# Early input columns at the seam of two blocks, a slot of its own for the lanes' change of tokens, and GpSimd multiplying values with gates

## What is computed

```python
def peer_ffn_2(xn, w_q, sub_keys, u_tab, v_tab):
    ...
        eidx = jnp.take_along_axis(cidx, ci, axis=-1)     # 8 heads x 16 experts a token
        gate = jax.nn.softmax(cs, axis=-1)
        ug = u_tab[eidx]
        act = jax.nn.gelu(jnp.einsum('td,thkd->thk', xb, ug).astype(f32))
        vg = v_tab[eidx]
        return jnp.einsum('thk,thkd->td', (gate * act).astype(vg.dtype), vg)
```

```python
    lam = lax.complex(a_re.astype(f32), a_im.astype(f32))
    dt = jnp.exp(log_dt.astype(f32))[:, None]
    a_bar = jnp.exp(lam * dt)
    b_bar = ((a_bar - 1.0) / lam)[..., None] * lax.complex(b_re.astype(f32), b_im.astype(f32))
```

## Time and profile before

| | before |
|---|---|
| median of 3 runs | 1944.17 us |
| lowest, highest | 1938.46, 1945.6 us |
| profiled execution | 1944.28 us |
| its span on the core | 1942.4 us |
| PE busy | 1879.8 us (97%) |
| DVE busy | 1254.2 us (65%) |
| ACT busy | 495.9 us (26%) |
| POOL busy | 360.3 us (19%) |
| DMA | 619.66 MB, mean 319 GB/s |

### The profile page before, as it was taken

One profiled execution on the slowest core, in us unless ns is written; L12 is line 12 of the kernel. 1 busy time (PEld: TensorE's weight loads), 2 busy tenths in 40 slices (PEclk: granted clock), 3 DMA queues, 4 the chain that ended last, 5 costly groups with the idle time before them and its releaser, 6 DMA issues. The chain is left out here.

```text
span 1942.4 us, 33702 instructions
## 1 busy us (share of the span) xinstructions
PE 1879.8 (97%) x13111; PEld 1757.2 (90%) x13111; DVE 1254.2 (65%) x2927; ACT 495.9 (26%) x1707; POOL 360.3 (19%) x310
## 2 busy tenths in 40 slices
PE   8999999999999999999999989999999999999998
PEld 6877779999999999999988567899999999999998
DVE  6228566998888834434599974339997888444344
ACT  3013302324445310000311024013234454100002
POOL 0000000233333211111000740000332333111110
PEclk9999999999999999999999999999999999999999
DMA  7763369999999999999544120379999999999996
GB/s 307 279 253 128 135 257 371 361 415 414 414 415 414 406 391 414 413 413 414 198 137 145 66 98 1 109 273 349 417 415 414 413 414 414 390 414 413 414 413 242
DMA packets 125373, 619.66 MB, mean 319 GB/s; under 512 B 14812, under 2 KB 17020, under 8 KB 83360
## 3 DMA queue, kind: packets, MB, share of 16 engines
q1 hardware_dynamic: 91264, 382.77, 50.5%
q0 software_dynamic: 31376, 226.27, 28.6%
q10 hardware_dynamic: 2576, 8.48, 1.2%
HBM read 614.84 MB, written 2.62 MB: 318 GB/s over the span
## 5 line engine op out<-in xcount | busy, mean ns | idle before, releaser
L1237 PE MATMUL bank<-expert_coef,ring 128*128 128x152 f32 x4096 | 535.8, 293 | 5.2 <-DMA ring<-in_uv 4.6
L1237 PEld LDWEIGHTS bank<-expert_coef,ring 128*128 128x128 f32 x4096 | 530.4, 190 | 8.9 <-DMA ring<-in_uv 7.6
L1208 PE MATMUL bank<-h,ring 128*128 128x152 f32 x3712 | 498.9, 293 | 4.4 <-DMA ring<-in_ut 4.4
L1208 PEld LDWEIGHTS bank<-h,ring 128*128 128x128 f32 x3712 | 484.8, 190 | 6.2 <-DMA ring<-in_ut 6.0
L1156 POOL DMA_INDIRECT expert_rows<-in_uv,pair_index x208 | 289.4, 1391 | 971.1 <-DVE pair_sum L1528 534.5
L1517 DVE CUSTOM_DVE_ANT_0 expert_rows<-expert_rows,h_tokens 128x1024 f32<-128x1024 f32 x192 | 234.4, 1221 | 213.6 <-DMA expert_rows<-in_uv,pair_index 213.5
L1528 DVE SCALAR_TENSOR_TENSOR pair_sum<-expert_rows,pair_coef,pair_sum 128x1024 f32<-128x1024 f32 x192 | 246.2, 1282 | 45.9 <-ACT pair_coef L1378 44.6
L1376 ACT ACTIVATE pair_act<-pair_dot 128x1 f32<-128x1 f32 x208 | 42.2, 203 | 599.4 <-DVE pair_dot L1517 599.1
L1172 PE MATMUL bank<-h,ring 128*128 128x128 f32 x1024 | 117.1, 275 | 0.0
L1172 PEld LDWEIGHTS bank<-h,ring 128*128 128x128 f32 x1024 | 116.0, 192 | 0.1
L1362 ACT ACTIVATE work<-work,choice 128x128 f32<-128x128 f32 x304 | 97.2, 406 | 0.0
(11 more groups left out here) (414 smaller groups left out, 2058.1 us busy)
## 6 DMA issues: line engine op xcount, KB each, us to landing
ring<-in_uv SPq DMA_DIRECT2D x256, 512.0 KB, 13.1
ring<-in_ut SPq DMA_DIRECT2D x232, 512.0 KB, 14.7
ring<-in_dense SPq DMA_DIRECT2D x92, 1024.0 KB, 4.8
expert_coef<-in_ut SPq DMA_DIRECT2D x24, 512.0 KB, 8.0
ada<-in_ada SPq DMA_DIRECT2D x8, 1024.0 KB, 23.8
ada_late<-in_ada ACTq DMA_DIRECT2D x7, 1024.0 KB, 4.7
ada_late<-in_ada SPq DMA_DIRECT2D x5, 1024.0 KB, 11.8
ada<-in_ada POOLq DMA_DIRECT2D x4, 1024.0 KB, 16.1
```

Of the source, the lines that this page charges most:

```text
L1208: ins = nc.tensor.matmul(k.bank[e % 4][:, 0:DENSE], w[:, kk, :], k.h[:, kk, SPREAD_END:TOK], start=kk == 0, stop=kk == KD - 1)
L1237: ins = nc.tensor.matmul(down_bank(i), w[:, i * P:(i + 1) * P], A[:, e, :], start=e == 0 and i % 3 == 0, stop=e == NB - 1, skip_group_chec ...
```

## The change

It does four things.

1. **Front columns at the seam.** In place of the products that feed nothing, TensorE multiplies the 116 front columns for the first four tiles of the second block's input projection (`EARLY_TILES`), in banks 2 to 5, at the end of `peer_layer` "1". In `block2_inputs` the first four tiles then cover only the other 156 columns.
2. **The S5 factors in layer 1.** Their constants come by a transfer on ScalarE's queue, and their arithmetic (one Exp, two Sin, one Tanh on ScalarE; a chain on VectorE in three parts) is put between late pairs in the down half of layer 1. What `block2_inputs` still does of it are the masks, the input factors, and the tables.
3. **A slot for the turn.** The change of tokens at p = 32 gets a step of its own, `turn_at` = 69, without a pair. Every pair from 32 on comes two tiles later, so `late` becomes 61. The last four pairs before the gates move to other tiles (`PAIR_AT`: 45, 46, 48, 50 become 45, 47, 51, 53). In the down half a gather waits for 59/20 = 2.95 tiles more instead of 3.
4. **GpSimd multiplies.** `weigh` goes from VectorE's program to GpSimd's, where the multiplies that are due stand between the issues of the gathers (`weigh_to`). ScalarE waits for all of them before it widens the first shared tokens.

```diff
+EARLY_TILES, EARLY_BANK = 4, 2
-PAIR_AT = (3, 5, 7, 9, 11, 13, 15, 17, 19, 22, 24, 26, 28, 30, 32, 34, 36, 38, 40, 42, 45, 46, 48, 50)
+PAIR_AT = (3, 5, 7, 9, 11, 13, 15, 17, 19, 22, 24, 26, 28, 30, 32, 34, 36, 38, 40, 42, 45, 47, 51, 53)
...
-    pairs_in = lambda e: range(EARLY_PAIRS + max(0, e - GATES_FROM) // 2, EARLY_PAIRS + max(0, e + 1 - GATES_FROM) // 2)
+    turn_at = GATES_FROM + 1 + 2 * (Q - EARLY_PAIRS)
+
+    def pairs_in(e):
+
+        if e <= GATES_FROM or (e - GATES_FROM) % 2 == 0 or e == turn_at:
+            return []
+        return [EARLY_PAIRS + (e - GATES_FROM) // 2 - (1 if e > turn_at else 0)]
...
-    late = EARLY_PAIRS + (NB - GATES_FROM) // 2
+    late = EARLY_PAIRS + (NB - GATES_FROM) // 2 - 1
...
+                def weigh(e):
+
+                    t = filled[e]
+                    pool.wait_ge(k.geld.sem, k.geld.at(e + 1))
+                    pool.wait_ge(k.evicted.sem, k.evicted.at(t // GROUP))
+                    nc.gpsimd.tensor_tensor(A[:, e, 0:t], tmp[:, e % 3, 0:t], A[:, e, 0:t], ALU.mult)\
+                        .then_inc(k.weighed.sem, 1)
...
                 for p in range(NS):
+                    if p - BUFFERS + 1 > EARLY_PAIRS:
+                        weigh_to(next((e for e in range(GATES_FROM, NB) if p - BUFFERS + 1 in pairs_in(e)), NB) if p - BUFFERS + 1 < late else NB)
...
                     if p > late + 1:
-                        pool.wait_ge(k.w_used.sem, k.w_used.at(3 * (p - late - 1)))
+                        pool.wait_ge(k.w_used.sem, k.w_used.at(59 * (p - late - 1) // 20))
...
                 if not last:
-                    pe.wait_ge(k.rooted.sem, k.rooted.at(1))
-                    keep_busy(k, 14, k.bank[4][:, 0:TOK], k.const[:, 0:TOK])
+                    next_front = slice(0, META + FRONT)
+                    pe.wait_ge(k.front_scaled.sem, k.front_scaled.at(1))
+                    for j in range(EARLY_TILES):
+                        c = NC2 + NR + NB + j // 2
+                        if j % 2 == 0:
+                            arrived(k, pe, c)
+                        w = chunk(k, c).rearrange("p (k n) -> p k n", k=KD)
+                        for kk in range(KD):
+                            nc.tensor.matmul(k.bank[EARLY_BANK + j][:, next_front], w[:, kk, (j % 2) * P:(j % 2 + 1) * P],
+                                             k.h[:, kk, next_front], start=kk == 0, stop=kk == KD - 1)
...
                 act.wait_ge(k.gated.sem, k.gated.at(NGROUPS))
+                act.wait_ge(k.weighed.sem, k.weighed.at(len(mixed)))
                 widen(0)
+                if s5 is not None:
+                    act.dma_start(par, k.args["s5_par"]).then_inc(k.s5_par_dma, 16)
                 for p in range(late, NS):
+                    if s5 is not None and p == late + 8:
+                        act.wait_ge(k.s5_par_dma, 16)
+                        nc.scalar.activation(scratch[:, 0, :], par[:, 2, :], ACT.Exp).then_inc(k.s5_stepped.sem, 1)
+                    if s5 is not None and p == late + 11:
+                        act.wait_ge(k.s5_angled.sem, k.s5_angled.at(1))
+                        nc.scalar.activation(s5.phs[:, 1, :], scratch[:, 2, :], ACT.Sin)
+                        nc.scalar.activation(scratch[:, 3, :], scratch[:, 2, :], ACT.Sin, scale=0.5)
+                        nc.scalar.activation(scratch[:, 1, :], scratch[:, 1, :], ACT.Tanh).then_inc(k.s5_turned.sem, 1)
...
                 def pair(p):
 
-                    if p:
+                    if p and p != Q:
                         add(p - 1)
...
-                    elif p % Q == 0 and p <= NP:
+                    elif p % Q == 0 and Q < p <= NP:
                         dve.wait_ge(k.added.sem, k.added.at(p))
                         turn(p // Q)
...
-                    if e - 1 in mixed:
-                        weigh(e - 1)
+                    if e == turn_at:
+                        add(Q - 1)
+                        dve.wait_ge(k.added.sem, k.added.at(Q))
+                        turn(1)
                     for p in pairs_in(e) if e < NB else ():
                         pair(p)
...
                 for p in range(late, NS - 1):
                     pair(p)
+                    if s5 is not None and p == late + 9:
+                        s5_angles()
+                    if s5 is not None and p == late + 12:
+                        s5_rotation()
+                    if s5 is not None and p == late + 14:
+                        s5_factors()
...
-                        out = k.bank[j % BANKS][:, 0:TALL if j < NUX else TOK]
+                        out = k.bank[(j + EARLY_BANK) % BANKS][:, 0:TALL if j < NUX else TOK]
...
+                            if j < EARLY_TILES:
+                                out, right = out[:, META + FRONT:], k.h[:, kk, META + FRONT:]
...
-                act.wait_ge(k.s5_dma, 48)
-                nc.scalar.activation(tmp[:, 0, :], par[:, 2, :], ACT.Exp).then_inc(k.recip_ready.sem, 1)
...
-                pool.dma_start(par[:, :, :], k.args["s5_par"]).then_inc(k.s5_dma, 16)
...
-                dve.wait_ge(k.s5_dma, 48)
-                dve.wait_ge(k.recip_ready.sem, k.recip_ready.at(1))
-                ch.then(nc.vector.tensor_tensor(T(1), par[:, 0, :], T(0), ALU.mult))
...
+                dve.wait_ge(k.s5_dma, 32)
```

More of the change, by code:

```diff
@@ L1020, in project_and_square, with peer_layer @@
         sig.advance(KD)
-def peer_layer(k, layer, gelu, gate, gain, shift, out=None):
+def peer_layer(k, layer, gelu, gate, gain, shift, out=None, s5=None):
     nc = k.nc
@@ L1146, in _, with weigh_to @@
                 pool.wait_ge(k.listed.sem, k.listed.at(1))
+                def weigh(e):
[4 more added lines that the diff above has]
+                        .then_inc(k.weighed.sem, 1)
+                done = [0]
+                def weigh_to(e):
+                    while done[0] < len(mixed) and mixed[done[0]] < e:
+                        weigh(mixed[done[0]])
+                        done[0] += 1
                 for p in range(NS):
+                    if p - BUFFERS + 1 > EARLY_PAIRS:
+                        weigh_to(next((e for e in range(GATES_FROM, NB) if p - BUFFERS + 1 in pairs_in(e)), NB) if p - BUFFERS + 1 < late else NB)
                     if p == BUFFERS - 1:
@@ L1715, in _, with s5_angles @@
                 nc.vector.tensor_copy(pindex[:, NP:], placed[:, 0, :]).then_inc(k.listed.sem, 1)
+                step = lambda i: scratch[:, i, :]
+                def s5_angles():
+                    turn_of = 2 * math.pi
+                    p1 = float(np.float32(round(turn_of * 256) / 256))
+                    p2 = float(np.float32(round((turn_of - p1) * 2 ** 20) / 2 ** 20))
+                    p3 = float(np.float32(turn_of - p1 - p2))
+                    dve.wait_ge(k.s5_stepped.sem, k.s5_stepped.at(1))
+                    ch.then(nc.vector.tensor_tensor(step(1), par[:, 0, :], step(0), ALU.mult))
+                    ch.then(nc.vector.tensor_tensor(step(2), par[:, 1, :], step(0), ALU.mult))
+                    ch.then(nc.vector.tensor_scalar(step(3), step(2), 1 / turn_of, None, ALU.mult))
+                    ch.then(nc.vector.tensor_copy(whole[:, 0:S5G], step(3)))
+                    ch.then(nc.vector.tensor_copy(step(3), whole[:, 0:S5G]))
+                    for part in (p1, p2, p3):
+                        ch.then(nc.vector.scalar_tensor_tensor(step(2), step(3), -part, step(2), ALU.mult, ALU.add))
+                    for sign in (1.0, -1.0):
+                        ch.then(nc.vector.tensor_scalar(step(3), step(2), sign, math.pi, ALU.mult, ALU.is_gt))
+                        ch.then(nc.vector.scalar_tensor_tensor(step(2), step(3), -sign * turn_of, step(2), ALU.mult, ALU.add))
+                    ch.then(nc.vector.tensor_scalar(step(2), step(2), math.pi, -math.pi, ALU.min, ALU.max))
+                    nc.vector.tensor_scalar(step(1), step(1), 0.5, None, ALU.mult).then_inc(k.s5_angled.sem, 1)
@@ L1808, in peer_layer @@
         k.inverted.advance(2)
+        k.front_scaled.advance(1)
+    if s5 is not None:
+        for sig in (k.s5_stepped, k.s5_angled, k.s5_turned):
+            sig.advance(1)
         k.dense_squared.advance(KD)
@@ L1901, in _ @@
-                turn = 2 * math.pi
-                p1 = float(np.float32(round(turn * 256) / 256))
-                p2 = float(np.float32(round((turn - p1) * 2 ** 20) / 2 ** 20))
-                p3 = float(np.float32(turn - p1 - p2))
-                ch.then(nc.vector.tensor_scalar(T(3), T(2), 1 / turn, None, ALU.mult))
-                ch.then(nc.vector.tensor_copy(tmpi[:, :], T(3)))
-                ch.then(nc.vector.tensor_copy(T(3), tmpi[:, :]))
-                for part in (p1, p2, p3):
-                    ch.then(nc.vector.scalar_tensor_tensor(T(2), T(3), -part, T(2), ALU.mult, ALU.add))
@@ L2600, in build @@
          k.joined, k.landed, k.totalled, k.dense_squared, k.coded, k.placed,
-          k.widened) = (k.counters[n] for n in PEER_SIGNALS)
+          k.widened, k.front_scaled,
```

(5 more changed lines are left out.)

98 lines of the change are left out of this document (39 added, 59 removed).

## The result

The changed kernel takes 1930.78 us (median of 19 runs, 1928.32 to 1949.8) against 1943.58 for the kernel before (19 runs); the ratio is 0.9943 with the interval 0.9918 to 0.9967, so 6 to 16 us faster. 1934.3 was forecast, 1929 to 1941 its range.

The account below looks back on a forecast made before the run. TensorE and the DMA queues were both taken as full, so TensorE's waits were to be gained: -5.5 - 3.2 - 2.3 + 3.2 - 2.2 = -10.0 from 1944.28 us, forecast 1934.3 us, range 1929 to 1941.

Parts of the forecast that it names:

- Front columns and S5: Seam and second block's input stage: TensorE's 6.1 us less work counts, seam 0.6 longer; -5.5 us, bounds -6.1 and -4.3.
- The turn: Token change in both layers' gating part: TensorE's wait for ScalarE goes; -3.2 us, bounds -3.2 and 0.
- the widened tokens: Second shared tokens, both layers: an earlier gather start removes TensorE's waits of 0.6 and 1.3; -2.2 us, bounds -2.2 and 0.
- The multiplies: Gate multiplies moved from VectorE to GpSimd: 0, since TensorE wasn't waiting for VectorE outside the turn; bounds 0 and +22.
- The lock's rival: Gating part: each GpSimd multiply holds VectorE up, deciding from 0.57 us a multiply; 22 us slower, 1956; chance 0.07.
- One gather more: Down half: 41 instead of 40 gathers paced by down tiles, 1.6 a layer; +3.2 us, bounds 0 and +5.1.
- The slack of the change-over: Change from up to down, 680 to 700: rate falls to 359 GB/s, leaving 1.1 MB for the first gather's earlier start.
- The free-gather rival: Down half: the extra gather is swallowed by the change-over's slack and costs nothing; -13.2, 1931 us; chance 0.22.
- First gates: Before the first gates: ScalarE's dot wait shrinks, 1.2 us comes up at the third gate; -2.3 us, bounds -3.5 and 0.
- The bytes rival: Gating part: TensorE's saved waits may return as ring waits, each down half pays 2.5; -5.3, 1939; chance 0.20.

Follow-up runs that it names:

- e1: Changed kernel with the S5 factors worked out in the second block's input stage again, early front columns kept; ratio 1.0007 to the kernel before.
- e2: Changed kernel with the products that feed nothing back at the seam instead of the early front columns, S5 kept in layer 1; ratio 1.0004 to the kernel before.
- e3: Changed kernel with the token change inside pair 32 again and 40 paced gathers, one per 3 tiles, in the down half; ratio 0.9978 to the kernel before.
- e8: Kernel before with one edit: each paced gather of the down half may start two tiles sooner; ratio 1.0014 to the kernel before.
- e4: Changed kernel with the multiplies with the gates back on VectorE, at their old place; ratio 0.9956 to the kernel before.
- e7: Changed kernel with one more GpSimd multiply of 128 x 256 values behind each multiply with the gates; ratio 0.9942 to the kernel before.
- e10: Changed kernel with one gather in each layer's down half bringing 2 rows instead of 128; ratio 0.9939 to the kernel before.
- e5: Changed kernel with the last early pairs behind tiles 45, 46, 48 and 50 again; ratio 0.9959 to the kernel before.
- e11: Changed kernel with 8 TensorE passes that feed nothing behind up tiles 70 and 100 of each layer; ratio 0.9971 to the kernel before.
- e0: The changed kernel once more, no edit, as measure for the others; ratio 0.9953 to the kernel before.
- e9: Changed kernel with each paced gather of the down half two tiles sooner; ratio 0.9955 to the kernel before.
- e6: Changed kernel with two gathers in each layer's down half bringing 64 rows instead of 128; ratio 0.9965 to the kernel before.

## Why the prediction was right

The range held the time and the direction was right. By its steps:

- **Front columns and S5, -5.5.** Right to a tenth: 0.7 longer at the seam (0.6 forecast) and 6.2 shorter in the stage. e1 and e2 show the reason given for it, that TensorE and VectorE had arrived together.
- **The turn, -3.2, and the widened tokens, -2.2.** The waits went as told, and come back with e3. What they were worth wasn't separated from the gather's place: e3 undoes all three, and e8's earlier gathers end the wait for widened tokens too.
- **The multiplies, 0.** Right (e4), and with room to spare (e7). The lock's rival is out. The longest multiply was put at 0.45 by its columns; those of 140 columns took 0.55, which cost nothing either.
- **One gather more, +3.2.** This step failed. It took bytes and products to be balanced along the down half and charged 1.6 a layer. e3, which undoes turn, widened tokens and gather together, costs 5.5 and not 2.2. The two waits could give 5.4 at most, by the forecast's own prices, so nothing is left for the gather to cost, within about 1 us. The slack of the change-over, 1.1 MB by the earlier trace rows, was mentioned and took only 0.1 off the 1.7 a layer; in fact the change-over carries 1.12 MB more in layer 1 (28.62 against 27.50), about one gather. The free-gather rival had the mechanism. That it also had the time, 1931, is partly luck, for its sum holds the -2.3 of the first gates. Whether a gather in the balanced part costs its 2.5 stays open (e10: yes in layer 2, no in layer 1).
- **First gates, -2.3.** This step failed too. The wait was as long as told, and 0.9 came up at the third gate where 1.2 was forecast, but undoing the edit costs nothing (e5). The bytes rival had the mechanism: what TensorE loses there the loads gain. It looked for the return as longer waits for the ring in the up half; it came as a longer down half.

So the layers gave 6.6 (3.6 + 3.0, with the means) where -3.2 - 2.3 + 3.2 - 2.2 = -4.5 was forecast; with the 5.5 of the seam 12.1 instead of 10.0. Two wrong terms of opposite sign, +3.2 and -2.3, account for 0.9 of the difference; 1.2 is within what single profiles leave to chance. That the two nearly cancel is luck, though with either alone put right the forecast, 1931 or 1936.6, would have been inside the range too.

Open: how much of the 6.6 is TensorE's wait at the turn and how much the place of the gathers. By the idle time 4.7 lies at the change-over, e8 gets 2.4 by earlier gathers (which by the prediction's prices may be the widened tokens' waits alone), and of a delay in the up half nothing (e5) or between a third and two thirds (e11) remains. No run takes the turn's wait away and leaves the gathers where they were.

## What to carry to other kernels

Where an engine and the queues are both full, don't add up the engine's waits: ask of each edit whether the queues stand idle for less time, and look for the stretches where the rate falls below its plateau, because a transfer put there cost nothing here, and of a wait elsewhere only a part, or nothing, remained where the loads could run ahead. Where two engines arrive together at the end of a stage, cost the edits as a pair; undoing either one left nothing of the gain here. Terms smaller than the whole time's interval can still be read from stage lengths, if several kernels share the stage.

## What the hardware showed that was not expected

From VectorE's first S5 product to the first up product of layer 2 the same program took 303.4 us in the changed kernel's profile, 290.1 in e0 and 282.3 in e2: the granted clock of 1150 to 1200 was 0.77, 0.85 and 1.00, and in the first TensorE's lower level (1.2 GHz) ruled part of the next 50 us too (0.75). These 21 us are more than the whole change brings.

The clock also fell inside the layers, where TensorE is nearly always busy: right behind waits of 2.0 to 2.9 us in the up half of layer 1 it stood at 0.66 or 0.67 over 5 us in e4, e5, e8 and e10, and in e4 that left 28 passes of 42. A wait of 2.0 at 487 in e9 had no such fall behind it. So a wait can cost TensorE more than its length; yet the sums of e4's and e5's layers with it, 587.3 and 586.4, are those of the changed kernel (586.6).

A gather of 64 rows held the queues at least as long as one of 128 (e6: 320 GB/s over 10 us at a busy share of 1.02, and 172 to 238 GB/s in the half-microsecond slices from 723.5 to 727.5). The Trainium skill (SBUF — State Buffer, "Door 1: The DMA port swizzle") has a transfer to the first 64 partitions reach half of the ports; a rate of about half of 414 in these slices agrees.
